# Between the router and the gathered experts: gates dealt out among the tiles, banks and parts in order of first use, group numbers read one by one

## The reference

```python
def merge_branches(y_hy, y_gla, y_att, br_g, P):
    g_hy, g_gla, g_att = jnp.split(br_g, N_BRANCH, axis=-1)
    m = (jax.nn.sigmoid(g_hy) * (y_hy @ P['w_br_hy'])
         + jax.nn.sigmoid(g_gla) * (y_gla @ P['w_br_gla'])
         + jax.nn.sigmoid(g_att) * (y_att @ P['w_br_att']))
    return m @ P['w_out']

def grouped_moe(h, router_w, router_b, w_gate, w_up, w_down):
    ht = h.reshape(-1, shape[-1])
    scores = jax.nn.sigmoid((ht @ router_w).astype(f32))
    sel = scores + router_b.astype(f32)
    group_score = lax.top_k(sel.reshape(-1, N_GROUPS, EXPERTS_PER_GROUP), TOP_K)[0].sum(-1)
    group = jnp.argmax(group_score, axis=-1)
    in_group = (jnp.arange(N_EXPERTS) // EXPERTS_PER_GROUP)[None, :] == group[:, None]
    _, idx = lax.top_k(jnp.where(in_group, sel, -jnp.inf), TOP_K)
    w = jnp.take_along_axis(scores, idx, axis=-1)
    w = w / jnp.sum(w, axis=-1, keepdims=True)
    gates = jnp.sum(jax.nn.one_hot(idx, N_EXPERTS, dtype=f32) * w[..., None], axis=1).astype(h.dtype)
    for e in range(N_EXPERTS):
        hid = jax.nn.silu(ht @ w_gate[e]) * (ht @ w_up[e])
        out = out + gates[:, e:e + 1] * (hid @ w_down[e])
    return out.reshape(shape)

    # in the block: shift2, scale2 and gate2 are columns of silu(c) @ w_mod + b_mod
    x = x + gate1[:, None, :] * y
    h = modulate(rms_norm(x, norm2_g[l]), shift2, scale2)
    x = x + gate2[:, None, :] * grouped_moe(h, router_w, router_b, moe_w_gate[l], moe_w_up[l], moe_w_down[l])
```

## Time and profile before

| | us |
|---|---|
| median of 3 runs | 1798.01 |
| lowest and highest of them | 1794.42, 1799.25 |
| the profiled execution | 1799.21 |
| its span in the trace | 1797.3 |
| PE busy, of the span | 1662.2 (92%) |
| DVE busy | 1100.5 (61%) |
| ACT busy | 867.3 (48%) |
| mean DMA rate | 166 GB/s |

### The profile page before, as it was taken

One profiled execution on the slowest core, in us unless ns is written; L12 is line 12 of the kernel. 1 busy time (PEld: TensorE's weight loads), 2 busy tenths in 40 slices (PEclk: granted clock), 3 DMA queues, 4 the chain that ended last, 5 costly groups with the idle time before them and its releaser, 6 DMA issues.

```text
span 1797.3 us, 23022 instructions
## 1 busy us (share of the span) xinstructions
PE 1662.2 (92%) x9782; PEld 1414.6 (79%) x9782; DVE 1100.5 (61%) x1328; ACT 867.3 (48%) x1004; POOL 8.6 (0%) x19
## 2 busy tenths in 40 slices
PE   6999999999999898999899987899998997899998
PEld 3788868698986676878798766699996885799986
DVE  5567563435455687976456567666556657665555
ACT  5554543644434676765244345454444437354443
POOL 0000000000000000000000000000000000000000
PEclk9899999889989899999999988999999998899999
DMA  6636302125643798987454313255544441445540
GB/s 224 218 96 230 112 21 73 47 94 155 236 151 129 256 338 300 355 314 254 165 189 165 130 48 117 95 188 187 188 165 163 142 164 40 146 166 189 186 164 24
DMA packets 132381, 297.69 MB, mean 166 GB/s; under 512 B 5207, under 2 KB 16776, under 8 KB 131320
## 3 DMA queue, kind: packets, MB, share of 16 engines
q1 hardware_dynamic: 130192, 287.93, 46.5%
q0 software_dynamic: 1184, 5.72, 1.0%
q10 hardware_dynamic: 904, 2.58, 0.4%
HBM read 295.17 MB, written 1.05 MB: 165 GB/s over the span
## 4 chain that ended last, share of the span: by engine, by line
PE 78%; DVE 12%; ACT 7%; issue 1%; DMA 1%; ACTq 0%; POOL 0%; DVEq 0%
PE bank L437 77%; DVE cut L1398 3%; ACT cut L2325 2%; PE bank L450 1%; ACT arena L2524 1%; DVE stat L1612 1%; ACT pairs L2331 1%; DVE XT L2193 1%; DVE pairs L2200 0%; DVE XT L2187 0%; ACT arena L2533 0%; DVE stat L2173 0%; DMA arena<-in_posemb 0%; DVE arena L1419 0%; DVE XT L2170 0%
## 5 line engine op out<-in xcount | busy, mean ns | idle before, releaser
L1398 DVE TENSOR_TENSOR cut<-raw,cut 128x2048 fp32r<-128x2048 f32 (+1 forms) x268 | 605.8, 2275 | 413.2 <-ACT cut L2325 412.5
L437 PE MATMUL bank<-pairs,cut 128*128 128x256 f32 (+1 forms) x5480 | 693.1, 288 | 24.1 <-DVE cut L1398 10.6
L437 PEld LDWEIGHTS bank<-pairs,cut 128*128 128x128 f32 (+1 forms) x5480 | 681.2, 193 | 34.9 <-DVE cut L1398 17.7
L2325 ACT ACTIVATE cut<-raw 128x2048 fp32r<-128x2048 f32 (+1 forms) x268 | 505.7, 1899 | 363.9 <-PE bank L437 349.0
L437 PE MATMUL bank<-cut,pairs 128*128 128x512 f32 (+1 forms) x2460 | 595.3, 402 | 28.9 <-DVE cut L1398 11.1
L437 PEld LDWEIGHTS bank<-cut,pairs 128*128 128x128 f32 x2460 | 467.4, 194 | 146.5 <-issue 23.4
L437 PE MATMUL bank<-arena 128*128 128x128 f32 (+10 forms) x748 | 189.2, 417 | 24.2 <-DMA arena<-in_posemb 7.2
L437 PEld LDWEIGHTS bank<-arena 128*128 128x128 f32 (+4 forms) x748 | 113.3, 200 | 80.4 <-issue 57.1
L2331 ACT ACTIVATE pairs<-arena 128x256 fp32r<-128x256 f32 (+1 forms) x81 | 37.4, 496 | 88.2 <-DVE arena L2237 51.5
L450 PEld LDWEIGHTS bank<-cst,arena 128*128 128x128 f32 x264 | 34.1, 155 | 43.6 <-DVE arena L1623 16.0
L450 PE MATMUL bank<-cst,arena 128*128 128x128 f32 x264 | 45.0, 305 | 21.8 <-DVE arena L1623 11.6
(11 more groups left out here) (291 smaller groups left out, 893.4 us busy)
## 6 DMA issues: line engine op xcount, KB each, us to landing
raw<-in_moe_w_gate SPq DMA_DIRECT2D x32, 1024.0 KB, 7.4
raw<-in_moe_w_up SPq DMA_DIRECT2D x32, 1024.0 KB, 6.5
raw<-in_moe_w_down SPq DMA_DIRECT2D x32, 1024.0 KB, 6.7
raw<-in_w_in SPq DMA_DIRECT2D x30, 1024.0 KB, 5.2
raw<-in_w_mod SPq DMA_DIRECT2D x24, 1024.0 KB, 5.3
raw<-in_ffn_w_gate SPq DMA_DIRECT2D x22, 1024.0 KB, 5.1
raw<-in_ffn_w_up SPq DMA_DIRECT2D x22, 1024.0 KB, 5.1
raw<-in_ffn_w_down SPq DMA_DIRECT2D x22, 1024.0 KB, 5.0
```

What stands on the lines that cost most here:

```text
L437: return pe.matmul(o, l, r, start=start, stop=stop, skip_group_check=True)
L1398: v.tensor_tensor(both[:, PIECE:PIECE + n], M.raw[K.place(i)[0]][:, 0:n], both[:, 0:n].bitcast(F32), ALU.subtract).then_inc(*up("lo_w", i))
L2325: a.activation(M.cut[K.slot(i)][:, 0:n], M.raw[K.place(i)[0]][:, 0:n], ACT.Copy).then_inc(*up("hi_w", i))
```

## The change

Seven edits, all between the branch projections and the first slot expert.

1. The high and low parts of the first two pairs of `YA` are cut before the branch `gl` is merged, no longer after it; `router_factors` moves with them on DVE, ahead of `gl`'s merging.
2. The router's shift is multiplied and summed over k on DVE (`RSH`, `RSS`), and PE sums it over the partitions with one matmul.
3. `mod_whole`: block 10 is given out as 1, 5 and 2 k-steps, and all eight of block 11, now in bank 0, come before `gather`.
4. `tokens_lo` works in halves of 512 columns, the first halves earlier and the last after `places`; ACT's `tokens_hi(0)` moves into `features`.
5. `gather`'s tiles take banks 4, 5, 6, 7, 2, 3, 6, 7, so that bank 4, which `slot_half(0, 0)` needs, holds the first tile; `slots` is split in `way_back` (run between the two weight pieces of `slot_half(0, 0)`) and `slot_gates`.
6. `gates` is split in five parts that stand between the calls of `gathered`; the first and the second expert piece are cut before tiles 3 and 6 (before: the first alone, before tile 4).
7. SP reads one group number before the first MoE weights, and each other one when it first needs it.

```diff
-        P.wait_ge(*K.load("rw", 3))
-        P.wait_ge(*at("mod", 1))
-        chain(o[:, 0:16], [(M.mod[:, 24 + k, 0:1].broadcast_to([128, 128]), M.RWT[:, k, :])
-                           for k in range(8)]).then_inc(*up("crw"))
+        P.wait_ge(*at("RSS"))
+        mm(o[:, 0:16], C("ones"), M.RSS, True, True).then_inc(*up("crw"))
...
     def gather():
-        for i in range(2):
-            P.wait_ge(*at("lo", "H2T", i))
         P.wait_ge(*at("P"))
         for k in range(8):
-            o = claim(("gx", k), ("fg", k), (2, 3, 4, 5, 6, 7))
+            for i in range(2):
+                P.wait_ge(*at("lo", "H2T", i, k // 4))
+            o = claim(("gx", k), ("fg", k), ((4, 5, 6, 7, 2, 3, 6, 7)[k],))
...
-    mod_whole(10, 0, 2)
     turn_half(1, 1)
     route(1, 0)
-    mod_whole(10, 2, 1)
+    mod_whole(10, 0, 1, 1)
     route(1, 1)
-    mod_whole(10, 3, 5)
+    mod_whole(10, 1, 5, 1)
     counts()
-    mod_whole(11, 0, 5)
+    mod_whole(10, 6, 2, 1)
+    mod_whole(11, 0, 8, 0)
     gather()
-    mod_whole(11, 5, 3)
...
-            slot_half(u, 0)
+            slot_half(u, 0, way_back if u == 0 else lambda: None)
             if u:
                 slot_turn(u - 1)
             else:
-                slots()
+                slot_gates()
                 spread()
...
         w(*K.load("rw", 3))
+        v.tensor_tensor(M.RSH, M.RWT, long(M.mod[:, 24:32, 0], 16), ALU.mult).then_inc(*up("v"))
+        w(*at("v"))
+        v.tensor_reduce(M.RSS, M.RSH.rearrange("p k e -> p e k"), AX.X, ALU.add).then_inc(*up("RSS"))
...
+    for j in range(2):
+        attended_lo(j)
+    router_factors()
     for br, name in ((1, "gl"), (2, "at")):
         if br == 2:
-            router_factors()
-            for j in range(4):
+            for j in (2, 3):
+                attended_lo(j)
...
-    tokens_lo(0)
+    tokens_lo(1, 0)
     largest()
     places()
-    tokens_lo(1)
-    for k in range(4):
-        gathered(k)
+    for b in range(2):
+        tokens_lo(b, 1)
+    v.tensor_tensor(M.RRd, wide(C("ident"), 2), long(RS2, 128), ALU.mult).then_inc(*up("rrd"))
+    group_only()
+    gathered(0)
+    largest_gate()
+    gathered(1)
+    second_gate()
+    gathered(2)
     cut_until(first + 1)
-    for k in range(4, 8):
-        gathered(k)
-    gates()
+    gathered(3)
+    both_gates()
+    gathered(4)
+    gathered(5)
+    cut_until(first + 2)
+    gathered(6)
+    gathered(7)
+    gates_out()
...
-            groups = [sp.value_load(M.IDX[0:1, s:s + 1], min_val=0, max_val=3) for s in range(4)]
+            groups = {}
+        if p.place is not None and p.place not in groups:
+            groups[p.place] = sp.value_load(M.IDX[0:1, p.place:p.place + 1], min_val=0, max_val=3)
```

52 lines of the change are left out of this document (31 added, 21 removed).

## The result

| | before | after |
|---|---|---|
| median, runs | 1794.48 us, 5 | 1783.27 us, 5 |
| lowest and highest | 1792.89, 1799.25 | 1778.60, 1785.57 |
| profiled execution, its span | 1799.21, 1797.3 | 1783.27, 1781.5 |

The account below looks back on a forecast made before the run. It took the stretch as bound by PE's work where PE is busy and by the chain ACT, DVE, PE in the gaps. Gains 2.97 + 2.3 + 1.0 + 4.0 = 10.3 us, from 1799.21 to 1788.9 us; range 1784.8 to 1793.5.

Parts of the forecast that it names:

- The two terms, 2.97 and 2.3: Branch `at`: 2.97 us of PE idleness removed, plus 2.3 us as the 192 matmuls behind it keep full clock.
- The clock's term: Behind the gap before `at`: full instead of half rate for 192 matmuls, 2.3 us, bounds 0 and 2.3.
- Paid back here: Counts to gather: counts come 1.7 us earlier, but PE's ten k-steps of `mod_whole` start the gather 0.8 us later.
- The sum: Whole kernel: 2.97 + 2.3 + 1.0 + 4.0 = 10.3 us gained, giving 1788.9 us.
- rival C: Second piece of `slot_half(0, 0)`, perhaps behind it: PE keeps full clock, 2.4 us; 1786.5 or 1785 us; chance 0.10.
- the upper bound of the text, 6.4: Gather to `slot_half(0, 1)`: largest gain allowed, 6.4 us, if the clock is full in the second piece.
- the 4.0 that went into the sum: Gather to `slot_half(0, 1)`: second piece 2.25 us earlier, plus `way_back`'s 1.7 us moved into PE's idle time.
- Rival B: `slot_half(0, 0)`: `way_back` blocks PE longer than it frees, so 4.0 us is lost; 1792.9 us; chance 0.11.
- Rivals A: Branch `at`: the clock falls all the same, by another gap, losing 2.3 us; 1791.2 us; chance 0.13.
- D: From 605 us on: weight stream bounds, SP's three reads add 2.3 us, PE's gain given back; 1801.5 us; chance 0.04.
- E: Following experts: their waits absorb the gain, so it doesn't arrive; 1799 us; chance 0.05.

Follow-up runs that it names:

- early_cut_alone: Before with only the first two pairs of `YA` and `router_factors` moved ahead of the branch `gl`; median 1788.67 us (4 runs), ratio to before 0.9948.
- no_early_cut_again: After with the four parts of `YA` cut behind `gl` as in before, executed a second time; 1784.08 us (1 run).
- after_third: The changed kernel, unaltered, measured a third time; median 1783.82 us (6 runs).
- x_mods: After with four k-steps of block 11 moved, two ahead of the gather's last tile and two behind the gather; 1779.43 us (5 runs), ratio to before 0.9915.
- three_behind: After with the last three k-steps of block 11 put behind the gather again; 1786.23 us (1 run).
- cut_and_shift: Before with only the early `YA` cut and the router's shift summed on DVE; median 1786.84 us (10 runs), ratio to before 0.9967.
- x_mods_behind: After with four k-steps of block 11 inside or behind the gather and `way_back` behind the first half; 1781.19 us (6 runs), ratio to before 0.9899.
- no_early_cut: After with the four parts of `YA` cut behind `gl` as in before; median 1787.92 us (7 runs), ratio to before 0.9958.

## Why the prediction was wrong in size and right in direction

**Edit 1** held in all its steps. PE has no gap, the delayed weight piece was covered, and the clock stays at 1.00. The two terms, 2.97 and 2.3, make 5.27; at the router's shift 5.8 us were gained (before to early_cut_alone) and 5.1 (no_early_cut_again to after_third), and in the stretch 5.0 and 5.15. The clock's term was short by 0.55 in the first pair: the prediction took 34.7 us for 288 matmuls and the same mean for the other 192, 57.8 us in all, and the run of 480 takes 57.2.

**Edit 2** gave 1.07 us for 1.0, by the way the prediction told: w_out waits for ACT's second copy.

**Edit 3**: counts 1.77 us earlier for 1.7, and from them to the gather 2.0 us more for 2.5. The twenty passes took 8.27 us to the gather's start (556.22 to 564.49) for 8.6. "Paid back here" is confirmed by x_mods and three_behind.

**Edits 4 to 6** up to the second piece: 17.51 us behind the gather, against 591.5 - 574.1 = 17.4. The first piece waited for the low part of its weights and the second for `RSB`, as forecast. Undoing the banks costs 2.8 us, undoing the dealt gates 4.3 us.

**Edit 7**: 0, measured as 0. The reads were 0.26 to 0.47 us each, wherever they stood. The Trainium skill, page "DMA: Bandwidth & Descriptors", section "Latency and other measured facts", gives such a read a floor of about 600 ns, which would speak against dealing them out; the trace has 270 to 470 ns for the instruction itself, and no cost of the dealing shows in the rest, 1192.1 us dealt and 1192.3 us grouped.

**The step that failed is the clock, priced in one place of three.** The sum has the granted clock behind the gap that the change removes, and only there. The second place is the second piece of `slot_half(0, 0)`. I had its row, 0.54, and even its price, 2.4 us, but put it into rival C with a chance of 0.10. It came to 2.2 us, and it is there in seven of eight executions with after's order of work (2.86 to 2.89 us from the second piece to the gates, once 4.42). By comparison of like with like (cut_and_shift and after_third, both with the slower w_out) edits 3 to 7 are worth 135.14 - 128.65 = 6.5 us. That is the upper bound of the text, 6.4, and not the 4.0 that went into the sum. The third place, w_out, was in no case at all: the sum and every rival put it at nothing without a reason, though before's trace has a clock of 0.70 from 530.4 to 536 us. It is 1.5 us in the executions that escape it.

Setting these beside the sum: 10.2 us for the stretch, 0.55 more behind the gap, 1.5 in w_out, 2.2 in the second piece and 0.2 in the remaining small terms make the 14.7 measured. The other 1.1 us between the spans lie outside the stretch, 0.7 ahead and 0.4 behind it, and belong to the executions. So the 5.6 us by which the profiled execution beat the forecast are 4.5 us of clock and small terms in the stretch and 1.1 us outside it. That two of these (1.5 and 1.1) come or stay away with the single execution is luck of the pair of traces; the 2.2 us of the second piece is not. Rival B was wrong in its result and right in its mechanism (`way_back` holds up the second piece by 2.6 us, and gives 1.8 us back). Rivals A, D and E are out: the clock did not fall in `at`, and the rest of the kernel took neither the 2.3 us of D nor the gain back.

What remains open is why the clock is at its full rate in the second piece in after and not in x_mods, where the first piece had it (3.36 us for the first, 4.58 us for the second; after 5.49 and 3.04). In the four executions with before's order both pieces are slow (4.35 to 4.58 and 5.25 to 5.49 us). In each of the 13 others only one is: the first in nine, the second in four (three_behind, x_mods, x_mods_behind, and once no_early_cut, whose order here is after's). In after it fell on the one behind which PE waits for ACT anyway. Undoing the banks, the dealt gates, the reads or the place of `way_back` left the second piece at its full rate; it lost it in the three kernels that put k-steps back behind the gather. The runs show that it falls so, not why. The two short executions behind `slot_half(0, 1)` are open in the same way: both have `way_back` behind the half and both had the full clock from 392 to 404 us. Eight executions with that clock and without that order, and the one with that order and a low clock there, took the long rest; whether the two together are what it takes, two executions don't show.

## What to carry to other kernels

In this kernel the removed gap of 2.97 us had cost its own length and 2.85 us of half rate behind it, and the gap of 3.38 us that no_early_cut brings back costs 1.7 us on top. So price a removed gap with a clock term between half of its length and all of it, read from the rows behind it. Then put a price on the granted clock in every stretch that the edit moves, not only behind the gap that it closes, and give the case in which they are all at the full rate a real chance. And compare traces from a common start, step by step: executions of this kernel differ by 7.5 us ahead of the change, which hides an edit of 1 us in the medians and not in the stretch.
